# Gated delta rule of a hybrid decoder trunk: another order of work on four engines, and one of two stores moved to another engine's queue

## The reference, cut to what matters

```
kb = kc * bc[..., None]
L = jnp.where(strict, jnp.einsum('bhnid,bhnjd->bhnij', kb, kc) * decay, 0.0)
T = lax.linalg.triangular_solve(eye + L, ...)          # the inverse of I + L
u = T @ (vc * bc[..., None]);  w = T @ (kb * jnp.exp(g)[..., None])
a_intra = jnp.where(tril, jnp.einsum('bhnid,bhnjd->bhnij', qc, kc) * decay, 0.0)
def step(state, xs):
    v_new = u_i - w_i @ state
    o_i = (q_i * jnp.exp(g_i)[..., None]) @ state + a_i @ v_new
    state = state * jnp.exp(g_last) + (k_i * jnp.exp(g_last - g_i)).T @ v_new
...
o = rms_norm(o, o_norm) * jax.nn.silu(gate)
```

## Time and profile before

| | us |
|---|---|
| median of 3 runs | 3547.83 (3542.74 to 3550.08) |
| the profiled execution | 3547.12 |
| its span | 3545.4 |
| outside the span | 1.7 |
| the delta rule stage in it | 720.0 to 974.9 |

### The profile page before, as it was taken

The page is one execution under the profiler, slowest core; times in us unless marked ns, Lnnn a source line. Parts: engine busy times, 40 slices in busy tenths (PEclk is TensorE's granted clock), DMA queues, the critical chain, the costliest instruction groups (busy, mean ns, idle before and its releaser), DMA issues. The chain is left out here.

```text
span 3545.4 us, 42696 instructions
## 1 busy us (share of the span) xinstructions
PE 3189.5 (90%) x14997; PEld 1738.4 (49%) x14998; DVE 1243.7 (35%) x3007; ACT 882.7 (25%) x1714; POOL 617.2 (17%) x1035
## 2 busy tenths in 40 slices
PE   8987979947797999999889999999989969989886
PEld 6665764437643344334356666666644434333332
DVE  5665654445335122212242222332222231222224
ACT  1022224313312111111044444454430111111111
POOL 0000000047411111212121111111110101122213
PEclk9888999967798999999999999999989979999998
DMA  7730001122134898998541110011031157899975
GB/s 291 264 122 4 0 10 32 42 59 57 31 133 179 354 368 354 410 397 365 196 161 36 36 36 28 9 36 36 1 121 37 34 236 312 318 425 425 412 321 228
DMA packets 181625, 612.92 MB, mean 173 GB/s; under 512 B 54637, under 2 KB 105544, under 8 KB 148462
## 3 DMA queue, kind: packets, MB, share of 16 engines
q1 hardware_dynamic: 159118, 566.97, 41.4%
q0 software_dynamic: 22080, 42.01, 3.1%
q10 hardware_dynamic: 288, 2.10, 0.2%
HBM read 592.59 MB, written 52.99 MB: 182 GB/s over the span
## 5 line engine op out<-in xcount | busy, mean ns | idle before, releaser
L1897 PE MATMUL ret_pqkv<-ret_w,hT_mix 128*128 128x512 f32 x1024 | 452.9, 595 | 2.0 <-PEq L2637 2.0
L2470 PE MATMUL f0e_pgu<-f0w_gu,f0e_xT 128*64 128x512 f32 x1568 | 345.3, 596 | 8.4 <-issue 4.6
L1759 PE MATMUL mo_py<-mo_w,mixT 128*128 128x512 f32 x768 | 335.3, 597 | 5.4 <-DMA mo_w<-in_ret_w_out_dram 2.9
L2470 PE MATMUL f1e_pgu<-f1w_gu,f1e_xT 128*64 128x512 f32 x1344 | 296.6, 596 | 7.4 <-issue 3.6
L1897 PEld LDWEIGHTS ret_pqkv<-ret_w,hT_mix 128*128 128x128 f32 x1024 | 190.7, 191 | 218.3 <-issue 218.3
L1759 PEld LDWEIGHTS mo_py<-mo_w,mixT 128*128 128x128 f32 x768 | 146.0, 192 | 187.2 <-issue 178.9
L2470 PEld LDWEIGHTS f0e_pgu<-f0w_gu,f0e_xT 128*64 128x64 f32 x1568 | 123.9, 138 | 224.5 <-issue 224.5
L1905 PE MATMUL ret_pgate<-ret_w,hT_mix 128*128 128x256 f32 x1024 | 231.6, 379 | 0.0
L2489 PE MATMUL f1e_pd<-f1w_d,f1e_hidT 128*64 128x512 f32 x672 | 167.5, 650 | 42.9 <-DMA f1w_d<-in_moe_w_down_dram 41.2
L1905 PEld LDWEIGHTS ret_pgate<-ret_w,hT_mix 128*128 128x128 f32 x1024 | 189.6, 190 | 23.6 <-issue 0.5
L2470 PEld LDWEIGHTS f1e_pgu<-f1w_gu,f1e_xT 128*64 128x64 f32 x1344 | 106.1, 138 | 192.6 <-issue 192.5
(11 more groups left out here) (562 smaller groups left out, 4723.2 us busy)
## 6 DMA issues: line engine op xcount, KB each, us to landing
f0w_gu<-in_moe_w_gate_dram SPq DMA_DIRECT2D x32, 2048.0 KB
f0w_gu<-in_moe_w_up_dram SPq DMA_DIRECT2D x32, 2048.0 KB
f0w_d<-in_moe_w_down_dram SPq DMA_DIRECT2D x64, 1024.0 KB
f1w_gu<-in_moe_w_gate_dram SPq DMA_DIRECT2D x32, 2048.0 KB
f1w_gu<-in_moe_w_up_dram SPq DMA_DIRECT2D x32, 2048.0 KB
f1w_d<-in_moe_w_down_dram SPq DMA_DIRECT2D x64, 1024.0 KB
mixT<-in_ada_w_dram SPq DMA_DIRECT2D x80, 512.0 KB, 5.6
ret_w<-in_ret_w_in_dram SPq DMA_DIRECT2D x16, 1024.0 KB, 9.8
```

Of the source, the lines that this page charges most:

```text
L1759: mm = pe.matmul(py[t % 3][:, half * 512:(half + 1) * 512], mixT[:, kk, t * P:(t + 1) * P], ws[:, kk, half * 512:(half + 1) * 512], start= ...
L1897: mm = pe.matmul(p_qkv[s % 2][:, :], g.hT[:, kk, t * P:(t + 1) * P], w[h % 2][:, kk, 0:512], start=(kk == 0), stop=(kk == KD - 1))
L2470: mm = pe.matmul(pgu[s][half * HALF:(half + 1) * HALF, :], xT[u % 2][:, kk, s * HALF:(s + 1) * HALF], ew.gu[u][:, :, kk, half * FH:(half + ...
```

## The change

All of it is in `delta_rule`. No computation is added or left out, and the sizes are the same.

- SyncE: `low_parts(it + 3)` now stands ahead of `inverse_out(it + 2)`, and `low_in(it + 3)` ahead of `inverse_in(it + 2)`. `inverse_out` stores `X` alone.
- ScalarE: the 8 DMAs that store `XT` are now issued by ScalarE (`turned_out`), behind the first `products` of a turn. `squares`, `decays`, `output` come behind the second `products`, `values` and `corner` behind the third, and `roots` behind them.
- TensorE: the key scores lead the turn, and `tokens` moves from near its start to between `last_first` and `last_second`; `read_out` and `added` come ahead of the second `second_products`, `output_turn` behind it.
- VectorE: `key_products` leads the turn; `differences` stands in its middle, `keys` near its end.
- The waits of `tokens` and of the key scores follow that order (`atd` two higher; `kdecd` and `vd` one lower).

```diff
@@ SyncE
             for it in TURNS:
+                if valid(it + 3):
+                    low_parts(it + 3)
                 if valid(it + 2):
                     inverse_out(it + 2)
                 if valid(it + 3):
-                    low_parts(it + 3)
+                    low_in(it + 3)
                 if valid(it + 2):
                     inverse_in(it + 2)
-                if valid(it + 3):
-                    low_in(it + 3)
...
@@ TensorE
-                wait("atd", 2 * b)
+                wait("atd", 2 * b + 2)
...
-                    wait("kdecd", b + 1)
-                    wait("vd", b + 1)
+                    wait("kdecd", b)
+                    wait("vd", b)
...
+                if valid(b):
+                    scores(b, 4, "ltm")
                 if valid(l):
                     first_products(l, 0)
                 if valid(r):
                     predicted(r)
-                if valid(b):
-                    tokens(b)
                 if valid(l):
                     second_products(l, 0)
...
                 if valid(l):
                     first_products(l, 1)
-                if valid(r - 1):
-                    output_turn(r - 1)
-                if valid(b):
-                    scores(b, 4, "ltm")
                 if valid(r):
                     read_out(r)
                     added(r)
-                if valid(l):
-                    second_products(l, 1)
                 if valid(b):
                     scores(b, 0, "atm")
                 if valid(l):
+                    second_products(l, 1)
+                if valid(r - 1):
+                    output_turn(r - 1)
+                if valid(l):
                     last_first(l)
+                if valid(b):
+                    tokens(b)
+                if valid(l):
                     last_second(l)
@@ ScalarE
+            def turned_out(c):
+                b = c % 2
+                if c >= 2:
+                    act.wait_ge(inv_in[b], 32 * (c // 2))
+                act.wait_ge(S["turnedx"], c + 1)
+                for k in range(8):
+                    act.dma_start(blocks(1, b, k), XT[b][H * k:H * k + H, :, :]).then_inc(inv_out[b], 16)
...
@@ VectorE
+                if valid(b):
+                    key_products(b)
                 if valid(r):
                     residual(r)
-                if valid(b):
-                    keys(b)
                 if valid(l):
                     updates(l, 0)
                 if valid(r):
                     new_values(r)
-                if valid(b):
-                    key_products(b)
+                if valid(b + 1):
+                    differences(b + 1)
                 if valid(r):
                     carried(r)
+                if valid(b):
+                    query_products(b)
                 if valid(l):
                     updates(l, 1)
                 if valid(r):
                     output_sum(r)
                 if valid(b):
-                    query_products(b)
+                    keys(b)
                 if valid(r):
                     output_norm(r)
-                if valid(b + 1):
-                    differences(b + 1)
```

More of the change, by code:

```diff
@@ L1029, in delta_rule, with blocks @@
         TURNS = range(-4, NT + 1)
+        def blocks(n, b, k):
+            at = B * (k % 4)
+            return d.inv_dram[n][b][B * k:B * k + B, :].rearrange("j (h c) -> h j c", c=64)[:, :, at:at + B]
         @block.sync
@@ L1066, in inverse_out @@
                     sp.wait_ge(inv_in[b], 32 * (c // 2))
[L1067 to L1072, removed]
+                sp.wait_ge(S["solved"], c + 1)
+                for k in range(8):
+                    sp.dma_start(blocks(0, b, k), X[b][H * k:H * k + H, :, :]).then_inc(inv_out[b], 16)
             def inverse_in(c):
@@ L1379, in _ @@
                     products(l, 0)
+                if valid(it + 2):
+                    turned_out(it + 2)
+                if valid(l):
+                    products(l, 1)
+                if valid(r):
+                    squares(r)
+                if valid(b + 1):
+                    decays(b + 1)
+                if valid(r - 1):
+                    output(r - 1)
+                if valid(l):
+                    products(l, 2)
                 if valid(b):
@@ L1382, in _ @@
                 if valid(l):
[L1383 to L1389, removed]
+                    corner(l)
                 if valid(r):
                     roots(r)
-                if valid(l):
-                    corner(l)
-                if valid(b + 1):
-                    decays(b + 1)
                 if valid(l + 1):
```

## The result

The changed kernel took 3557.62 us (median of 9 runs, 3550.42 to 3566.36), the kernel before, run beside it, 3546.80 us (9 runs, 3540.34 to 3550.08). The ratio is 1.0036, with an interval of 1.0023 to 1.0050: slower, by 10.8 us. The forecast was 3557.

What follows compares the result with a forecast made beforehand. No engine was full: a turn was a ring of waits. An early gain of 16.6 us, lost with 4.0 more in longer gated turns, and a longer tail left +9.5: 3547.1 to 3556.6, median 0.7 higher, forecast 3557 us, range 3543 to 3573.

Steps and rivals of the forecast that it cites:

- The start: Stage's beginning, before any gate: LT begins 2.7 us earlier because key scores no longer wait behind the transposes.
- the gain of 16.6 us: Saving over the first inverses, before any gate: third XT copy at 783.5 against 800.1.
- T2: Third mark, where GpSimd copies XT after an inverse: forecast at 783.5, against 800.1 before.
- The steady turn: Gated turns: ScalarE waits at its stores until the inverse ends, roots and gate follow; 30.6 us against 25.8.
- T: Mark from which a turn is counted: the end of one inverse, where GpSimd copies XT.
- Edits with no term: Moved differences, values, keys, low_parts, Sd and Td: hidden by waits; cover gone, each at most 1 to 4 us a turn.
- The sum: Whole program: profiled execution 3547.1 plus 9.5 gives 3556.6; median 0.7 higher, so 3557 us, +0.26%.
- the tail: Stage's end, after the last mark: first product copy at 17.5 us instead of 12.5; stage ends at 984.4, against 974.9.
- Rival 1: SyncE's and ScalarE's simultaneous stores hinder each other: 2 us in six turns, 12 us, giving 3569; chance 0.20.
- Rival 2: TensorE doesn't lose its clock for that long: 3.3 us shorter, a turn 27.3, giving 3541; chance 0.16.
- Rival 3: Next inverse doesn't wait for the gate: turn keeps 25 to 26 us, about 3537 to 3541; chance 0.03.
- Rival 4: Copies and roots overlap with waits added in series: turn of 28 to 29, 3547 +- 4, no change; chance 0.13.

Runs made afterwards that it cites:

- the fastest kernel: Changed kernel with SyncE storing X and XT, differences right behind the key products, roots ahead of values and corner: 3513.15 us, 0.9921 of before.

## Why the prediction was right, and where it was not

**The start and the gain of 16.6 us: right.** T2 came 63.4 us after the stage's start (63.5 forecast).

**The steady turn: the mechanism right, the size 0.8 us too large.** The list against the turn of T5 = 879.73:

| from T, us | forecast | measured |
|---|---|---|
| stores end | 3.9 | 3.6 |
| second copy | 4.5 | 4.3 |
| second products | 8.3 | 8.0 |
| last_first | 11.2 | 10.5 |
| third copy | 11.9 | 11.1 |
| corner | 14.6 | 13.2 |
| roots | 17.7 | 16.3 |
| next mark | 30.6 | 29.4 |

A store took 0.37 us, as SyncE's did, and not the 0.40 of ScalarE's other DMAs. The larger part is the clock: I had it at half up to `tokens`, and it rose within `last_first` (1.52 us), so `tokens` took 1.09 instead of 1.6. In the turn of T6 it stayed low longer (the transposes of `tokens` took 1.97 us), the stores took 3.69 us, and the turn 32.2. The mean of the four is 29.8 (30.6 forecast). What decides between the two courses the traces don't tell.

**"Edits with no term": the step that failed.** The differences were costed at nothing because VectorE waits at that place by my list of a steady turn, and steady turns bear it out (2.93 to 3.20 us). But I checked only the steady turn, and turn -1 has no `new_values` and late second products; there the differences start at T1. I had the row of 7.39 us and let it reach "3 us past T". In fact they started at T and lasted to T + 9.1, with `AT`, an update and `last_first` behind them. They cost TensorE its lead: the next key scores began 2.7 us ahead of T2 where the kernel with early differences has 7.2. Turn 0 so began at half clock (1.97 us for the first products at 788.13, where the kernel with early differences takes 1.15), though the prediction had it at full clock, with no idle TensorE ahead. Then turn 0's own differences, 3.20 us, stood ahead of the second updates as well. By the rows, the second copy of a product came 4.0 us later behind T2 than with early differences (7.8 us against 3.7), and from it to the gate it took 2.6 us more. The turn from T2 took 5.4 us more than forecast, and 6.7 more than with the differences moved. That this is the cause was shown by moving them: in every turn, and the interval is 26.4 us; in turn -1 alone, and the next ones meet the joins, 34.4 us. In the same paragraph the push on SyncE's `X` was too small as well: with the late key scores its stores began 6.5 us behind T2, not 1 to 2. The gate hid that, as forecast.

**The sum.** The stage is +12.3, not +9.5: +5.4 for the missed turn, -3.1 for the four turns, and +0.5 for the tail. The median's agreement within 1 us owes something to these errors having opposite signs, which is luck.

**Rival 1, two hindering queues: refuted.** 2.95 and 2.97 us at the same time; ScalarE's longest eight were 3.69, under the 4 us I had set, and SyncE's longest, 4.02, has its like in the kernel before, 3.99, where SyncE stored alone. The Trainium skill's rule in "DMA: Bandwidth & Descriptors", "Issuing engines are not separate DMA queues", that several issuers save only the sequencer's time, agrees with these rows. What the kernel shows beside it is what the saved time costs on the other queue.

**Rival 2, the clock stays: refuted for this kernel; its price was about right.** The clock did fall. Held up by filling, it gives 2.8 us a turn against this trace and 1.9 against that of the kernel with early differences, where I had 3.3.

**Rival 3, the gate isn't what the inverse waits for: refuted.** Only one inverse of the stage waited for `U`, the very first. From GpSimd's waits (what waited for what: us in all, times, longest):

```profile
POOL dr_y L1163 <- DVE dr_y L1489: 82.9, 8, 14.6
...
POOL dr_outer L1128 <- DMA dr_U<-gd_low: 12.5, 1, 12.5
```

**Rival 4, everything shifts less: refuted in sum.** One of the four steady turns (28.5 us) lay in its range of 28 to 29 and two within 0.4 us of it, but the turns from T2 and T6 did not, and the runs came out above its 3547 +- 4.

## What to carry to other kernels

A DMA that waits for a late producer doesn't belong into the queue of an engine whose next work is on the path of that same producer: the eight stores take 3 us to issue, and with the wait ahead of them ScalarE stood for 16. Measure what stands behind the wait before counting what the other queue saves. And an edit costed at nothing must be read in the first and last turns as well as in a steady one, since a pipeline's fill runs with another alignment.

Where two engines slow each other, a move cures one turn and can put the same collision into the next; the place must keep clear of the other engine in every turn. Here the early differences ended 1.1 us or more ahead of the next mark, in every turn of the three kernels that have them early throughout; no semaphore enforces it, so this too has to be read from the trace.

## What was not expected of the hardware

How sharply VectorE loses beside GpSimd. A group of instructions over the turn of T1, VectorE's differences and GpSimd's joins (line, operation, count: shortest, median, longest of one in ns):

```profile
L1495 DVE SCALAR_TENSOR_TENSOR dr_dec<-dr_dec,gd_gcol,future x8: 531/1416/1420, 769.5 to 778.1; 128x128 f32<-128x128 f32 x8
```

```profile
L1148 POOL TENSOR_TENSOR dr_LM<-dr_LT,dr_join x4: 1256/1263/1266, 772.7 to 776.7; 64x512 f32<-64x512 f32 x4
```

and the same line over the whole stage in the kernel with early differences:

```profile
L1495 DVE SCALAR_TENSOR_TENSOR dr_dec<-dr_dec,gd_gcol,future x64: 340/392/467, 728.1 to 863.0; 128x128 f32<-128x128 f32 x64
```

A difference beside a GpSimd instruction of 1.26 us takes 1.42 us, elsewhere 0.39; the joins take what they take without it (5.28 us for four, against 5.27 to 5.50). It is as if one difference got through for each GpSimd instruction. Key products of the same operation, with one operand in PSUM, took 2.15 us for eight beside the gate and the unit copy (at 896.68), and 2.16 beside the small instructions of an inverse. The Trainium skill says in "SBUF — State Buffer", "SBUF: two separate sides", that a VectorE instruction with two SBUF operands and a GpSimd instruction that reads SBUF exclude each other for the whole instruction. The differences read two SBUF operands, and VectorE's rows agree with it; on GpSimd's side no wait is to be seen.

In the fastest kernel the small scaling of the sums of squares (`dr_oss`, 128x8) took up to 1.26 us, where in the changed kernel it was 0.17 in all eight turns. The long one at 835.64 lies beside the joins of 834.26:

```profile
L1485 DVE TENSOR_SCALAR dr_oss<-dr_oss x8: 170/196/1262, 794.1 to 935.2; 128x8 f32<-128x8 f32 x8
```

That wasn't followed further.
